# The gate operand of the expert build laid out token by token

## The reference

```python
def one_block(xb):
    q = (xb @ w_q).reshape(blk, PEER_HEADS, 2, D_HALF)
    sc = jnp.einsum('thpd,hpnd->thpn', q, sub_keys)
    top_s, top_i = lax.top_k(sc, PEER_TOPK)              # 16 of 128 keys, twice per head
    ...                                                   # best 16 of the 256 pairs: idx, best_s
    gate = jax.nn.softmax(best_s, axis=-1)
    act = jax.nn.gelu(jnp.einsum('thkd,td->thk', exp_u[idx], xb))
    return jnp.einsum('thk,thkd->td', gate * act, exp_v[idx])
```

## Time and profile before

| | us |
|---|---|
| three runs | 3216.77, 3209.21, 3221.12; median 3216.77 |
| the profiled execution, its own time | 3211.92 |
| its span in the trace | 3210.1 |
| TensorE busy in the span | 2959.5 (92%) |
| VectorE busy | 2477.6 (77%) |
| GpSimd busy | 1012.0 (32%) |
| ScalarE busy | 813.1 (25%) |
| mean bandwidth of the transfers | 325 GB/s |

### The profile page before, as it was taken

One profiled execution on the slowest core, in us unless ns is written; L12 is line 12 of the kernel. 1 busy time (PEld: TensorE's weight loads), 2 busy tenths in 40 slices (PEclk: granted clock), 3 DMA queues, 4 the chain that ended last, 5 costly groups with the idle time before them and its releaser, 6 DMA issues.

```text
span 3210.1 us, 46711 instructions
## 1 busy us (share of the span) xinstructions
PE 2959.5 (92%) x17310; PEld 2582.6 (80%) x17310; DVE 2477.6 (77%) x5431; ACT 813.1 (25%) x2390; POOL 1012.0 (32%) x840
## 2 busy tenths in 40 slices
PE   8898999999999999977788978979999999999976
PEld 7797888888888888865666856869888888888865
DVE  2376799888888888877643776898888888888878
ACT  5332222222111111211354353222211112111112
POOL 5432122333323333333354321122322333332322
PEclk9898998999999999998877978989999999999988
DMA  5326778999999999999411356768999999999996
GB/s 186 98 91 247 266 300 315 372 422 421 422 422 419 417 419 415 413 415 420 161 58 53 98 188 253 271 242 318 406 422 422 421 422 421 416 417 420 411 419 279
DMA packets 159967, 1042.99 MB, mean 325 GB/s; under 512 B 18480, under 2 KB 23920, under 8 KB 44096
## 3 DMA queue, kind: packets, MB, share of 16 engines
q0 software_dynamic: 92160, 671.13, 51.4%
q1 hardware_dynamic: 63648, 357.59, 28.9%
q10 hardware_dynamic: 4000, 12.36, 1.1%
HBM read 1033.28 MB, written 7.86 MB: 324 GB/s over the span
## 4 chain that ended last, share of the span: by engine, by line
DMA 45%; PE 32%; DVE 13%; issue 7%; ACT 1%; POOL 1%; DVEq 0%; SPq 0%; ACTq 0%; POOLq 0%
DMA gata<-uvg,idxg 30%; DMA gatb<-uvg,idxg 14%; PE bank L514 7%; PE bank L711 7%; DVE acc L1619 6%; PE bank L501 3%; PE bank L503 3%; PE bank L502 3%; PE bank L698 2%; PE bank L600 1%; DVE gata L1611 1%; PE bank L531 1%; DMA U<-uvd 1%; PE bank L724 1%; PE bank L862 1%
## 5 line engine op out<-in xcount | busy, mean ns | idle before, releaser
L724 PE MATMUL bank<-a,V 128*128 128x256 f32 x4096 | 938.1, 389 | 78.6 <-DVE a L1602 70.5
L724 PEld LDWEIGHTS bank<-a,V 128*128 128x128 f32 x4096 | 798.1, 195 | 202.4 <-issue 77.9
L711 PE MATMUL bank<-xd,U 128*128 128x256 f32 x4096 | 941.3, 389 | 3.3 <-DMA U<-uvd 3.3
L1282 POOL DMA_INDIRECT gata<-uvg,idxg x428 | 501.1, 1171 | 1269.8 <-DVE acc L1619 1209.9
L711 PEld LDWEIGHTS bank<-xd,U 128*128 128x128 f32 x4096 | 790.9, 196 | 112.3 <-DMA U<-uvd 4.4
L1611 DVE CUSTOM_DVE_ANT_0 gata<-gata,xrow 128x1024 f32<-128x1024 f32 x428 | 522.1, 1220 | 226.7 <-DMA gata<-uvg,idxg 223.7
L1619 DVE SCALAR_TENSOR_TENSOR acc<-gata,wgt,acc 128x1024 f32<-128x1024 f32 x428 | 547.4, 1279 | 20.1 <-ACT wgt L1087 19.9
L1085 ACT ACTIVATE act<-dot 128x1 f32<-128x1 f32 x640 | 129.3, 202 | 1608.9 <-DVE dot L1611 1608.6
L1282 POOL DMA_INDIRECT gatb<-uvg,idxg x212 | 234.7, 1107 | 570.0 <-DVE acc L1619 560.2
L1611 DVE CUSTOM_DVE_ANT_0 gatb<-gatb,xrow 128x1024 f32<-128x1024 f32 x212 | 258.6, 1220 | 107.5 <-DMA gatb<-uvg,idxg 105.6
L698 PEld LDWEIGHTS bank<-B,oneA 128*128 128x128 f16 x4096 | 279.7, 150 | 34.0 <-DVE oneA L1585 15.4
(11 more groups left out here) (193 smaller groups left out, 2525.6 us busy)
## 6 DMA issues: line engine op xcount, KB each, us to landing
U<-uvd SPq DMA_DIRECT2D x128, 1024.0 KB
V<-uvd SPq DMA_DIRECT2D x128, 1024.0 KB, 9.1
raw<-lin SPq DMA_DIRECT2D x152, 512.0 KB, 3.6
gata<-uvg,idxg POOLq DMA_INDIRECT x428, 14.7
hsp<-h ACTq DMA_DIRECT2D x2, 2304.0 KB, 13.9
hx<-hsp SPq DMA_DIRECT2D x2, 2304.0 KB, 16.6
gatb<-uvg,idxg POOLq DMA_INDIRECT x212, 14.7
sk_g<-skT ACTq DMA_DIRECT2D x2, 1024.0 KB, 4.8
```

Source lines behind the costliest of these rows:

```text
L711: mm = pe.matmul(bank[s][:, TD * t:TD * t + TD], U[:, s, o:o + P], xd[:, k, :], start=(t == 0 and k == 0), stop=(k == DT - 1), skip_group_ ...
L724: mm = pe.matmul(bank[b][:, TD * (d % 2):TD * (d % 2) + TD], V[:, s, o:o + P], a[:, s, TD * k:TD * k + TD], start=(first and k == 0 and d ...
L1282: pool.indirect_dma_start(row(l, s), None, uvg[l], bass.IndirectOffsetOnAxis(idxg[:, s:s + 1], 0)).then_inc(g_in[s % SLOTS], 16)
```

## The change

The array `B` gets another layout. Before, the 16 tokens of a build were innermost and the 32 second keys outside them, so the 32 values that one matmul reads lay 16 elements (32 bytes) apart. Now each token's 32 values are side by side. TensorE's read of them (line 698) is contiguous; VectorE, which still computes with tokens innermost as `E` is laid out, writes its result with a step of 32 elements (64 bytes) from one to the next. `E`, `oneA` and all sizes stay. The instructions of every engine are the same, in the same order.

```diff
@@ -201,7 +201,7 @@
-        B = at_("B", 88064, [P, 2, 2, CHUNK, TB], F16)
+        B = at_("B", 88064, [P, 2, 2, TB, CHUNK], F16)
@@ -696,7 +696,7 @@
                 for t in range(TB):
                     for part in range(2):
                         mm = pe.matmul(bank[2 + s][:, CHUNK * t:CHUNK * (t + 1)], oneA[:, s, t // TG, :, t % TG],
-                                       B[:, s, part, :, t], start=(t == 0 and part == 0), stop=True,
+                                       B[:, s, part, t, :], start=(t == 0 and part == 0), stop=True,
                                        skip_group_check=True)
                 mm.then_inc(full[2 + s], 1)
@@ -1588,7 +1588,7 @@
                 dve.wait_ge(b_eq, NBLD * l + m + 1)
                 for part, v in enumerate((gh, gl)):
-                    ins = dve.tensor_tensor(B[:, s, part], E[:, s], v[:, None, t:t + TB].broadcast_to([P, CHUNK, TB]),
+                    ins = dve.tensor_tensor(B[:, s, part].rearrange("p t n -> p n t"), E[:, s], v[:, None, t:t + TB].broadcast_to([P, CHUNK, TB]),
                                             ALU.mult)
                 ins.then_inc(b_one, 1)
```

## The result

Four runs of the changed kernel took 3412.07, 3399.37, 3405.36 and 3407.84 us, median 3406.6; four of the kernel before on the same chip had a median of 3215.3 (3209.21 to 3221.12). The ratio is 1.0592, with an interval of 1.0577 to 1.0608. The forecast was 3219 us with a range of 3206 to 3248: what was called no change is a large loss, and the range missed it. The profiled execution of after took 3412.07 us, span 3410.3.

The account below looks back on a forecast made before the run. The loop was taken as DMA-bound at 419 GB/s, the lead-in as held by TensorE with VectorE close. 3211.92 + 2 x (1.5 + 1) = 3217 us, 3222 on the medians' scale; forecast 3219 in between, range 3206 to 3248.

Parts of the forecast that it names:

- the price of one write: VectorE, line 1591: each strided write of B costs 270 ns more, bounds 0 and 666 ns; 0.54 us per block.
- a longer end, not a slower stream: VectorE, line 1534: its strided f32 write's extra 99 ns lengthen only its end, so 270 ns was taken for B.
- The upper bound: VectorE's B write: line 1534's 99 ns paid per element, 0.77 ns each, gives 1079 ns, 666 ns more.
- What VectorE's work displaces: Extra VectorE work displaces waiting: lead-in 10.1 us, loop 122 us; cost 1.5 us per lead-in, 1 us per loop head.
- if the cover were gone: Loop: without waiting for gathers to hide it, VectorE's extra work would cost the whole 25 us per layer.
- The sign it had named for being wrong altogether: Loop: bandwidth falls while VectorE is under 90% busy, meaning a late VectorE starves the gathers.
- taken to stay at 64 ns: TensorE's builds, line 698: start-to-start time per matmul stays 64 ns, bounds 16 to 64; 56 ns would hardly matter.
- The load of oneA, taken as the limit: TensorE's builds: the strided stationary load, 150 ns against 98 side by side, is unchanged and keeps matmuls at 64 ns.
- (a): VectorE's strided 2-byte writes pay per element, 666 ns more each, mostly in the lead-in; slower, 3246 us; chance 0.24.
- (b): TensorE's moving read was the limit and TensorE paces the loop; 35 us less, 3177 to 3182 us; chance 0.06.
- (c): TensorE's builds gain but nothing follows; lead-in ends about a microsecond earlier; 3213 to 3218 us; chance 0.09.
- (d): VectorE's write keeps the packed rate and TensorE its 64 ns; no change, 3212 to 3217 us; chance 0.04.

Follow-up runs that it names:

- Experiment 4: Single VectorE multiplications and TensorE matmuls in several access patterns, put ahead of the kernel before; f16 writes 4, 8, 16 bytes apart took 718, 1333, 2644 ns.
- Experiment 3: Changed kernel, but VectorE goes token by token, reading E with a step of 16 elements and writing B side by side; 3236.84 us, 1.0071 of the kernel before.
- experiment 6: Kernel before with only the low part of B, one of the two writes, laid out token by token; 3256.62 us, ratio 1.0134.
- experiment 5: Kernel before with the new layout only in the lead-in's 17 blocks, 3323.58 us (1.0346), or only in the loop's 47, 3292.41 us (1.0238).
- experiment 7: Against the kernel before: E, B and oneA all token by token, written side by side, with token constants stored twice; 3197.84 us, ratio 0.9945.
- experiment 8: Against the kernel before: E and B token by token, written side by side with doubled constants, oneA unchanged; 3210.83 us against 3216.68, ratio 0.9982.

## Why the prediction was wrong

**The step that failed** is the first of its terms, the price of one write: 270 ns, with bounds of 0 and 666 ns. It is 1.80 us of VectorE's time in the mean (3.60 per block), and 1.99 and 2.22 us by the length of the instruction, in which the forecast had been reckoned. Two errors lie in it. The choice within the bounds rested on line 1537 starting 0.16 us before the end of line 1534, read as "a longer end, not a slower stream". Experiment 4 shows that such nanoseconds are paid per element, with a follower that starts the same 0.16 us early. The sign means nothing: in the changed kernel too the follower starts 0.39 us before the end of a write of 2.65 us. The upper bound came from an f32 write and was carried over per element, as if the width made no difference; nothing in the trace showed a 2-byte element written alone. So the bound from above was open, and an unknown of that kind needs more than 0.24 for the slow side.

**What VectorE's work displaces** was right. The prediction said that the lead-in is full after 10.1 us, that the excess is paid in full, that the loop hides up to its idle time, and that nothing is given back at the DMA cap. Put 1.80 us into its own sum: 2 x (17 x 3.60 - 10.1 + 47 x 3.60 - 125.4) = 190 us, so 3405 us on the scale of the medians (3215.3 for the kernel before on that chip), against a measured 3406.6. That price was measured in the result itself, so this tests the rest of the sum and not the forecast. Experiments 3 and 6 hit the lead-in to within 3 us at two other prices, 1.19 and 1.76 us per block, and experiment 5 shows the two stretches apart. For the loop the prediction wrote that if the cover were gone, the price would be the whole extra work. With 169 us in 125 it was gone, and the price was not the whole but the excess, 44 and 45 us. The sign it had named for being wrong altogether, a falling bandwidth with VectorE under 90% busy, did not come: the bandwidth fell to 396 GB/s with VectorE busy for 790.90 of 791 us.

**TensorE** was taken to stay at 64 ns and went to 59. The bounds (16 to 64, with 56 as a middle value) held, and so did the judgement that it hardly matters: 6 us of 3217 (experiment 8), all that shows of it in the lead-ins. The load of oneA, taken as the limit, is a limit of its own but not the only one; with either operand strided alone a matmul takes about 60 ns (experiment 4).

**The rivals.** (a) named the right mechanism, signs included: line 1591 far longer and gaps ahead of line 698 in the lead-in. Its price, 1.33 us per block, was little over a third of the real one, so its 3246 us, and the range that reached just over it, were too low by 160. Experiment 3, with 0.59 us per write, shows about what (a) as priced does: 3236.84 us, 18 us more than before where (a) had 31. (b) is refuted by experiment 7, where TensorE runs with 43 us of idle time and the loop keeps its length. (c) happened on TensorE and was buried under the writes; alone it is experiment 8. (d) is out. The 0.24 for (a) against 0.57 for the forecast was the wrong way round, and the rule of 16-byte lines that the prediction cited from the Trainium skill ("Advanced Engine Details and Errata", section "Memory Cachelines") against its own choice was the better witness for the writes.

## What to carry to other kernels

A layout that helps the engine that reads can cost the engine that writes far more: before turning an array round, look which element size lies innermost on the side that writes, and keep at least two f16 (here always one aligned 4-byte word) together there; a constant that is spread along the new inner axis can be stored twice to allow it. When the trace has no row for the new access pattern, a row of another element size is no upper bound; a few single instructions ahead of the kernel, as in experiment 4, would have given the price. And the price of more work on an engine that is not the bound is a threshold: its busy time per stage, less its idle time in that stage, told the lead-ins and loops here to within about 4 us at three different prices.

## What was unexpected of the hardware

- A multiplication of 512 f16 elements takes 420 ns written side by side and 2.4 to 2.6 us written one by one, at 16 bytes or any larger distance tried; for single elements the time goes with the number of 16-byte pieces entered, 5.2 ns each. f32 elements 16 bytes apart cost 1068 ns against 687. VectorE's forms with one input take 1493 ns where those with two take 2600.
- Scattered runs of two f16 take 591 ns, of four 418; the packed rate needs no longer run than two in the inputs either (421 ns in experiment 7).
- Reading with a step of 32 bytes costs VectorE 1058 ns for 512 elements, against 685 for the same walk side by side.
- TensorE takes 25 ns from one matmul of 32 columns to the next when both operands lie side by side, and 60 to 65 ns as soon as one of them is strided; the load of the stationary operand is 140 to 180 ns when it is strided (experiment 8) and 96 when it is not (experiment 7).
- GpSimd's starts of indirect transfers took 1559 ns in the mean beside the scattered writes, 1171 before, and 1190 in experiment 8. In the loop of after GpSimd still waits 306.5 and 125.3 us for VectorE, so no cost of this shows; why it is so was not tried.
